# A two-block transformer kernel: its last stage without GpSimd, and the ranks of an expert's rows spread over its places

## The reference

```python
h2 = rms_norm(x, ffn_norm)
g_idx = argmax(h2 @ w_router_group)              # one of 8 groups
top_p, top_i = top_k(softmax(e_logits[g_idx]), 2)  # 2 of its 8 experts
order = argsort(expert_id)                       # 2048 rows by expert, 64 experts
gate = ragged_dot(xs, w_gate, group_sizes)
up = ragged_dot(xs, w_up, group_sizes)
y = ragged_dot(silu(gate) * up, w_down, group_sizes)
x = x + zeros.at[tok].add(y * weights)
return rms_norm(x, final_norm)                   # x * rsqrt(mean(x*x) + 1e-6) * gain
```

## Time and profile before

| | us |
|---|---|
| three runs | 2075.22, 2075.54, 2076.32 |
| median | 2075.54 |
| the profiled execution | 2076.99 |
| its span, first to last instruction | 2075.3 |
| PE busy | 1934.8 |
| DVE busy | 781.3 |
| ACT busy | 669.2 |
| POOL busy | 619.7 |

### The profile page before, as it was taken

How to read it: one execution, slowest core, us unless ns; L and a number is a source line. 1 busy time by engine, 2 the same in 40 slices (tenths; PEclk the granted TensorE clock), 3 DMA queues, 4 the chain that set the end, 5 groups by cost and what they waited for, 6 DMA issues and landing times. The chain is left out here.

```text
span 2075.3 us, 31451 instructions
## 1 busy us (share of the span) xinstructions
PE 1934.8 (93%) x12039; PEld 1370.5 (66%) x12039; DVE 781.3 (38%) x1439; ACT 669.2 (32%) x1484; POOL 619.7 (30%) x674
## 2 busy tenths in 40 slices
PE   8999999999999999999999899999979888888885
PEld 7998887787787777888887767677653333333232
DVE  5233256666553454430112456566522111111114
ACT  5334145555323444331112433232213222222221
POOL 1226387242120110010104576665212112121111
PEclk9999999999999999999999999999999899999998
DMA  5104461211421145623332421211489999999987
GB/s 211 56 32 155 140 204 27 51 27 47 142 72 41 42 103 103 87 60 100 92 122 76 169 87 62 87 48 47 200 341 419 424 425 424 413 424 425 424 368 299
DMA packets 101622, 367.14 MB, mean 177 GB/s; under 512 B 18470, under 2 KB 41195, under 8 KB 74603
## 3 DMA queue, kind: packets, MB, share of 16 engines
q1 hardware_dynamic: 83632, 323.06, 43.2%
q0 software_dynamic: 16704, 42.10, 5.2%
q10 hardware_dynamic: 1146, 0.04, 0.0%
HBM read 320.98 MB, written 60.95 MB: 184 GB/s over the span
## 5 line engine op out<-in xcount | busy, mean ns | idle before, releaser
L2915 PE MATMUL ps<-w_gu,rows_t 128*64 128x512 f32 x1024 | 242.3, 628 | 28.7 <-DMA w_gu<-w_up 26.8
L2915 PEld LDWEIGHTS ps<-w_gu,rows_t 128*64 128x64 f32 x1024 | 74.8, 144 | 171.6 <-issue 142.2
L2934 PE MATMUL ps<-w_d,act_tt 128*64 128x512 f32 x512 | 127.6, 644 | 25.7 <-DMA w_d<-w_down 25.6
L3210 POOL DMA_INDIRECT y_d<-y_out,asg_i x32 | 32.5, 1015 | 378.2 <-DVE y_out L3019 378.2
L3010 DVE SCALAR_TENSOR_TENSOR act_g<-ps,rs_c,act_g 128x256 f32<-128x256 f32 x32 | 15.5, 484 | 286.6 <-ACT act_g L3001 286.6
L2355 PE MATMUL ps<-w_o,mix_t 128*128 128x512 f32 x256 | 123.0, 609 | 0.0
L1126 ACT ACTIVATE prob<-ps,stats 128x1024 f32<-128x1024 f32 (+7 forms) x128 | 94.5, 738 | 62.0 <-DVE stats L1089 61.7
L315 PE MATMUL ps<-tk_lo,h_hi 128*128 128x512 f32 x256 | 99.8, 390 | 0.0
L315 PE MATMUL ps<-tk_hi,h_lo 128*128 128x512 f32 x256 | 99.6, 389 | 0.0
L315 PE MATMUL ps<-tk_hi,h_hi 128*128 128x512 f32 x256 | 99.6, 389 | 0.0
L1089 DVE TENSOR_REDUCE stats<-ps 128x1 f32<-128x1024 f32 (+7 forms) x128 | 97.0, 758 | 4.4
(11 more groups left out here) (486 smaller groups left out, 4456.7 us busy)
## 6 DMA issues: line engine op xcount, KB each, us to landing
w_gu<-w_gate SPq DMA_DIRECT2D x64, 1024.0 KB, 19.5
w_gu<-w_up SPq DMA_DIRECT2D x64, 1024.0 KB, 22.4
w_d<-w_down SPq DMA_DIRECT2D x64, 1024.0 KB, 19.1
w_tk<-w_in SPq DMA_DIRECT2D x5, 2048.0 KB, 12.8
proj_d<-tok_o POOLq DMA_DIRECT2D x40, 256.0 KB, 2.3
tk_in<-proj_d SPq DMA_DIRECT2D x8, 1280.0 KB, 5.9
w_ch<-w_in SPq DMA_DIRECT2D x12, 512.0 KB, 9.9
proj_d<-conv_o POOLq DMA_DIRECT2D x12, 512.0 KB, 4.0
```

What stands on the lines that cost most here:

```text
L2915: mm = pe.matmul(ps[half, 2, :].rearrange("p (g n) -> p g n", g=2), rows_t[:, k, half], w_gu[q][:, h, :, k, :], start=(k == 0), stop=(k == ...
L2934: mm = pe.matmul(ps[half, 4 + j, :], act_tt[:, k, half], w_d[q][:, h, k, j * BANK:(j + 1) * BANK], start=(k == 0), stop=(k == 1))
L3210: pool.indirect_dma_start(out=y_d, out_offset=bass.IndirectOffsetOnAxis(ap=idx, axis=0), in_=y_out[q][:, :], in_offset=None, bounds_check= ...
```

## The change

It has three parts. First, `r_slot` comes from a third table of constants instead of from two DVE instructions: rank r of an expert now lies on place 4(r mod 8) + (r div 8) of its first 32 places, and ranks 32 to 63 likewise on the places 32 to 63. Ranks 0, 1, 2 lie on places 0, 4, 8. The table is loaded by one more small transfer of SP, and DVE's wait before it scales `w_r` takes five transfers instead of four.

Second, in the final stage SP waits for the scatters' own semaphores instead of `s_phase`, tiles 6 and 7 come by a transfer of 1 MB each, PE sums tile 6 instead of 7, and DVE adds tile 7.

Third, POOL has no part in it: ACT's square has scale 1/32 (so its sum is the mean), ACT takes the root of mean + eps, DVE the reciprocal. DVE's order is new. One root of a dummy value is taken ahead of the tiles.

```diff
+    half_row = np.arange(P) % HB
+    slot = half_row % 32 // 4 + 8 * (half_row % 4) + 32 * (half_row // 32) + NOWHERE * (np.arange(P) // HB)
+            sp.dma_start(r_slot[:, :], A["c_slot"]).then_inc(s_fg, 16)
-                    v.wait_ge(s_fg, 64)
+                    v.wait_ge(s_fg, 80)
-                v.tensor_scalar(r_slot[:, :], const("iota"), float(HB), NOWHERE - HB, ALU.is_ge, ALU.mult).then_inc(s_sum0, 1)
-                v.wait_ge(s_sum0, 2)
-                v.tensor_tensor(r_slot[:, :], r_slot[:, :], const("iota"), ALU.add).then_inc(s_sum0, 1)
-                v.wait_ge(s_sum0, 3)
+                v.wait_ge(s_sum0, 1)
...
-        ON_PE = (1, 3, 5, 7)
+        ON_PE = (1, 3, 5, 6)
-            wait(sp, s_phase, PH_M)
+            for q in range(NB):
+                wait(sp, s_sct[q], 16 * USES[q])
-            for i in range(1, T // 2):
+            for i in range(1, T // 2 - 1):
...
+            for t in (T - 2, T - 1):
+                sp.dma_start(yf[1][:, t - T // 2, :, :],
+                             y_d[t * 2 * P:(t + 1) * 2 * P, :].rearrange("(p k) n -> p k n", k=2)).then_inc((s_yf[3], s_yf7)[t - T + 2], 16)
...
+            v.memset(eps_f, EPS).then_inc(s_eps, 1)
             def last(t):
-                pool_f.wait(v, "rs", t)
+                act_f.wait(v, "root", t)
+                dve_rs.done(v.reciprocal(rsF[t], rtF[t]), "rs")
+                dve_rs.wait(v, "rs", t)
                 src = summed(t) if t in ON_PE else xf[:, t, :]
-            for t in range(T + 2):
-                if t < T and t not in ON_PE:
-                    add(t)
-                if t >= 2:
-                    last(t - 2)
+            add(0)
+            last(0)
+            add(2)
+            last(1)
+            last(2)
+            add(4)
+            last(3)
+            last(4)
+            last(5)
+            add(7)
+            last(6)
+            last(7)
...
+            act.wait_ge(s_eps, EPS0 + 1)
+            act.activation(stat_d[:, 25:26], eps_f, ACT.Sqrt, bias=eps_f)
...
-                act_f.done(act.activation(yf[t // 4][:, t % 4, 0, :], src, ACT.Square, accum_out=ssF[t % 4]), "sq")
-
-        def f_pool(pool):
-            for t in range(T):
-                act_f.wait(pool, "sq", t)
-                pool_f.done(pool.tensor_scalar(msF[t % 4], ssF[t % 4], 1.0 / D, EPS, ALU.mult, ALU.add), "ms")
-                pool_f.wait(pool, "ms", t)
-                pool_f.done(pool.tensor_tensor(rsF[t % 4], msF[t % 4], neghalf[:, 0:1], ALU.pow), "rs")
+                act_f.done(act.activation(yf[t // 4][:, t % 4, 0, :], src, ACT.Square, scale=D ** -0.5, accum_out=ssF[t]), "sq")
+                act_f.wait(act, "sq", t)
+                act_f.done(act.activation(rtF[t], ssF[t], ACT.Sqrt, bias=eps_f), "root")
```

More of the change, by code:

```diff
@@ L84, in constants @@
     cs = np.concatenate([np.cos(ang.astype(np.float64)), np.sin(ang.astype(np.float64))], axis=1)
-    return c.astype(np.float32), cs.astype(np.float32)
+    half_row = np.arange(P) % HB
+    slot = half_row % 32 // 4 + 8 * (half_row % 4) + 32 * (half_row // 32) + NOWHERE * (np.arange(P) // HB)
+    return c.astype(np.float32), cs.astype(np.float32), np.broadcast_to(slot, (P, P)).astype(np.float32)
 class Jobs:
@@ L1987, in build @@
         s_ldB = [sem(f"tk_in_in{p}") for p in range(2)]
-        s_wo2 = sem("w_o2_in"); s_wr = sem("rot_in"); s_gab = sem("gain_ab_in"); s_wos = sem("w_o2_scaled"); s_fg = sem("ffn_gains_and_w_r_in"); s_wrs = sem("w_r_scaled")
+        s_wo2 = sem("w_o2_in"); s_wr = sem("rot_in"); s_gab = sem("gain_ab_in"); s_wos = sem("w_o2_scaled"); s_fg = sem("ffn_gains_w_r_and_slots_in"); s_wrs = sem("w_r_scaled")
         s_res2 = [sem(f"res2_in{p}") for p in range(2)]
@@ L3267, in build @@
         fn2 = sb("fn2", [P, D], W_GU_AT[3])
-        ON_PE = (1, 3, 5, 7)
+        ON_PE = (1, 3, 5, 6)
         w_diag = sb("w_diag", [P, len(ON_PE), 2, P], W_GU_AT[3] + 4 * KB)
-        s_diag, DIAG0 = s_gdve, 10; s_fsum, FSUM0 = s_gact, 7; s_yf1, YF1 = s_win[1], 16
+        s_diag, DIAG0 = s_gdve, 10; s_fsum, FSUM0 = s_gact, 7; s_yf1, YF1 = s_win[1], 16; s_yf7, YF7 = s_win[2], 32; s_eps, EPS0 = s_cols, 2
         dve_f = Count("f_dve", "y0 y1", after=dve_n); dve_out = Count("f_out", "out", after=dve_a)
-        act_f = Count("f_act", "sq", after=act_n)
-        pool_f = Count("f_pool", "ms rs", after=pool_a)
+        act_f = Count("f_act", "sq root", after=act_n)
+        dve_rs = Count("f_rs", "rs", after=pool_a)
         s_out, OUT0 = s_qrst[0], 16 * T // 2
-        ssF, msF, rsF = ([stat_d[:, 8 * i + p:8 * i + p + 1] for p in range(4)] for i in range(3))
+        ssF, rtF, rsF = ([stat_d[:, 8 * i + t:8 * i + t + 1] for t in range(T)] for i in range(3))
+        eps_f = stat_d[:, 24:25]
         def f_sp(sp):
@@ L3313, in last @@
             def last(t):
-                pool_f.wait(v, "rs", t)
+                act_f.wait(v, "root", t)
+                dve_rs.done(v.reciprocal(rsF[t], rtF[t]), "rs")
+                dve_rs.wait(v, "rs", t)
                 src = summed(t) if t in ON_PE else xf[:, t, :]
-                dve_out.done(v.scalar_tensor_tensor(xf[:, t, :], src, rsF[t % 4], fn2[:, :], ALU.mult, ALU.mult), "out")
-            for t in range(T + 2):
-                if t < T and t not in ON_PE:
-                    add(t)
-                if t >= 2:
-                    last(t - 2)
+                dve_out.done(v.scalar_tensor_tensor(xf[:, t, :], src, rsF[t], fn2[:, :], ALU.mult, ALU.mult), "out")
+            add(0)
[10 more added lines that the diff above has]
+            last(7)
         def by_dve(t):
@@ L3332, in rows_in @@
                 eng.wait_ge(s_yf1, YF1 + 16)
+            elif t == T - 1:
+                eng.wait_ge(s_yf7, YF7 + 16)
             else:
@@ L3423, in _ @@
             moe_pool(pool)
-            f_pool(pool)
 _INS = ["x", "p", "positions", "norm_g", "mla_w_in", "mla_q_norm", "mla_w_q_b", "mla_kv_norm", "mla_w_kv_b",
@@ L3438 @@
     arrays = {name: np.ascontiguousarray(inputs[name]) for name in _INS}
-    arrays["c_table"], arrays["c_rot"] = constants()
+    arrays["c_table"], arrays["c_rot"], arrays["c_slot"] = constants()
     A = {name: nc.dram_tensor(name, a.shape, mybir.dt.from_np(a.dtype), kind="ExternalInput").ap()
```

## The result

The changed kernel takes 2059.80 us in the median of four runs (2059.24 to 2060.57), the kernel before 2075.38 (2074.34 to 2076.32): a ratio of 0.9922, 95% interval 0.991 to 0.9935. That is 15.6 us faster where 10.7 were forecast, and 0.7 us under the range. The sign and the main mechanism held; the size didn't. The profiled execution has a span of 2058.5, 16.8 under the one before, and the table cuts that at marks that both traces have. The profiles differ by 1.2 us more than the medians: the profiled execution before took 2076.99, 1.6 us over its median, the one after 2060.24, 0.4 over.

What follows compares the result with a forecast made beforehand. Transfers were taken as the bound, in the expert stage with some DMA engines behind by their rows, and in the final stage. Ranks and scatter 8.2, signal 1.2, final stage 1.3: 10.7 off 2075.5 gives 2064.8 us, range 2060.5 to 2071.

Steps and rivals of the forecast that it cites:

- What bounds the kernel, and the lag: End of expert stage: transfers set the pace; uneven rows put some DMA engines behind over 32 pairs, share 0.52 from 2000.
- `w_d` should land within 15 us: Sign in the profile afterwards: expert weight transfers of `w_d` land within 15 us of issue, where they took up to 24.7.
- Step 1, the ranks: End of expert weights: spread ranks even the engines; pair 31's product starts 8.3 us earlier, 9.2 with the `w_d` wait gone.
- The estimate by rows on the busiest engine: Expert stage: busiest engine goes from 164 rows to 131, mean 128; 11.1 us over the mean becomes 0.9, gaining 10.2.
- Step 2, the last scatter: Pair 31's scatter: issued at 2018.5, takes 7.5 us under load, lands at 2026.0, 8.2 us earlier than before.
- Steps 3 and 4, the signal and the final stage: After the last scatter: SP no longer waits for POOL, 1.2 us gained; the final stage's roots and order gain 1.3.
- The bound by the stores, L + 9.9: Final stage: stores queue behind `yf`, eight times 0.5 MB, ending no earlier than 9.9 us after L, the last `yf` landing.
- Roots and order: Final stage: roots on ACT, reciprocals on DVE and DVE's new order without a pause gain 1.3 us, between 0 and 2.5.
- 1: Expert stage: the change doesn't move the lag; only signal and final stage gain, 2.5 us, giving 2073.0; chance 0.07.
- 2: Expert stage's end: only the unused share comes back, PE takes the rest; 2068.5 us; chance 0.10.
- 3: Final stage on ACT: squares and roots change tables each time, sixteen loads, 11.7 us later, 2076.5; chance 0.03.
- Rival 4: Expert stage: engines take places in turn, busiest has 155 rows of mean 128, 8.4 us slower, 2081.4; chance 0.03.

Runs made afterwards that it cites:

- spread_alone: The kernel before with only the new places for the ranks; 2066.15 us, against 2075.91 for the kernel before in its session.
- clustered: The changed kernel with eight neighbouring ranks on four neighbouring places and the four that are 32 further on; 2099.58 us.
- two_apart: The changed kernel with neighbouring ranks two places apart instead of four; 2064.73 us.
- after_again: The changed kernel as it is, timed and profiled once more; 2060.37 us, ratio 0.9917 to the kernel before.
- late_pool: The changed kernel with one more GpSimd operation of one column that waits for the last root and that nobody needs; 2064.52 us.
- late_wait: The changed kernel with GpSimd only waiting for the last root, with no operation behind the wait; 2064.65 us.
- roots_alone: The kernel before with only ScalarE's roots and VectorE's reciprocals replacing GpSimd's part; ranks, order, transfers and waits as before; 2071.43 us.

## Why the prediction was wrong in size

*What bounds the kernel, and the lag.* Right, in mechanism and place. Some DMA engines were behind by their rows, the lag grew over 32 pairs, and spreading the ranks took it away (spread_alone, clustered, two_apart). No record names an engine; what shows it is that four placements landed in the order of the count and near its sizes. One of my signs for it was no sign: the landing time of `w_d`, up to 24.7 us, is mostly the weights that are queued ahead of it. In the changed kernel it is still 24.8 at most, with no lag left. So "`w_d` should land within 15 us" failed as a sign, though the mechanism was right. The unused share of the earlier trace rows was the row that told it.

*Step 1, the ranks.* I had 8.3 us for the start of pair 31's product and measured 9.6; with the wait for `w_d`, 9.2 against 10.0. I took three quarters of the `w_d` of pair 30 as done early by the engines ahead, and PE's pace from pair 30 as 15.3 us; it was 15.4, but its start came 9.7 us earlier instead of 8. The estimate by rows on the busiest engine (10.2, the one worked out beside the sum) was nearer than my own 8.3.

*Step 2, the last scatter.* It took 6.1 us from issue to landing, not 7.5: 6.5 before. With step 1 that makes 10.35 us where the sum had 8.2. Both misses go the same way. Over the profiles with spread and with ordered ranks it is 10.0 in the mean, so 1.8 of the miss is more than one profile's luck.

*Steps 3 and 4, the signal and the final stage.* 1.2 + 1.3 = 2.5 us forecast; 1.85 in the profile of the changed kernel (36.18 to 34.33 from landing to last store), 2.8 in the second one. The seven profiles with this final stage lie between 1.75 and 2.85. The size is right and the split isn't: I wrote that PE's copies are last in no wait, and in the profile of the changed kernel they head the chain. 9.93 us of copies, which began at a granted clock of 0.50 (the 1.2 GHz level), behind GpSimd's signal, hold tile 1's sum until 2038.6. The bound by the stores, L + 9.9, was right: 10.0 in after_again.

*The missing term.* This is the step that failed: "*Roots and order*" priced GpSimd's two operations by their length and stopped at the last product; from there to the end of the span, 7.6 us (2067.70 to 2075.3), I carried everything over as fixed. 2.6 of it is the last store, 0.4 the end itself, and the other 4.6 us were the drain of GpSimd. late_pool and late_wait put it back (4.7 and 4.3), roots_alone takes it away on the kernel before. With that term the forecast would have been 10.7 + 4.6 = 15.3 us, against 15.6 measured. That closeness is partly luck: between the profiles it is 10.35 + 1.85 + 4.6 = 16.8 where the sum would have had 8.2 + 2.5 + 4.6, and the medians differ by 1.2 less than the profiles.

*The rivals.* 1 is excluded by spread_alone (9.8 us from the places alone), 2 by spread_alone too (9.8 us, not some 5) and by the windows (no lag of PE took the rest), 3 by the one table load at 2015.46 and by ScalarE's roots of 0.3 us, 4 by two_apart and clustered. Rival 4 was also priced too high: it took the rows before as nearly even, but by places in turn the busiest engine has 144 there, so the change would have added 11 rows, 3.4 us by the same price, and not 8.4. By the Trainium skill, ScalarE: Activation LUTs, "What ACT_TABLE_LOAD costs", a switch has a drain beside the load; the load of the earlier trace rows has none behind it, and in the final stage one can't tell, since ACT had to wait for 7.0 us behind it anyway.

## What to carry to other kernels

In these runs, rows that are gathered or scattered by index went to a DMA engine by their partition, in groups of four and the four 32 further on. If the filled places are always the first ones, the busiest engine sets the pace. With 164 rows on it where the mean is 128, the profile showed that only where the issued work ran out, as a share that sinks slowly. Lay neighbouring ranks four places apart. And read a profile to its very end: name what every engine does between the last result and the end of the span. In this program GpSimd's last instruction is followed by 8.7 us of drain, which is free only if something else takes longer.

## What the hardware showed that I had not expected

- GpSimd's drain at the end of the program: 8.65 to 8.68 us from its last instruction, whether that is an operation (before, spread_alone, late_pool), a scatter's wait and the branches behind it (after) or a wait alone (late_wait). In before, spread_alone, late_pool and late_wait it was the last thing to end, 4.7 to 4.8 us behind the last store's landing; in the others the last store was.
- A share of 0.99 at 401 GB/s in clustered beside 1.01 at 425 in the changed kernel, from 1800 to 2000: with 256 rows on the busiest engine the uneven load shows as a loss of rate, hardly of share. With 164 rows (the kernel before, 1.01 at 424) it shows as neither.
- PE began its sixteen copies at a granted clock of 0.50 (1.2 GHz) in both kernels, after 9.1 us without work in the changed one and 9.5 in the one before. The copies took 9.93 us in the first, 5.7 of it at 0.50, and 8.62 in the second, 3.0 of it at 0.50; in after_again, behind 7.5 us without work, 8.86 and 3.5. So the sixteen copies of one kernel differ by over 1 us between two executions.
